# Twelve attention units laid out anew inside GEMM slots, with mask, peak and sink in one VectorE pass

## The reference, cut to what matters

```python
def swa_sink_attention(q, k, v, sinks):
    ...
    s = jnp.einsum('bnqhgd,bnkhd->bnhgqk', qb, kband).astype(jnp.float32) * (dh ** -0.5)
    ...
    s = jnp.where(valid[None, :, None, None, :, :], s, -jnp.inf)
    sink = sinks.astype(jnp.float32).reshape(Hkv, G)[None, None, :, :, None, None]
    m = jnp.maximum(jnp.max(s, axis=-1, keepdims=True), sink)
    p = jnp.exp(s - m)
    p = p / (jnp.sum(p, axis=-1, keepdims=True) + jnp.exp(sink - m))
    o = jnp.einsum('bnhgqk,bnkhd->bnqhgd', p.astype(v.dtype), vband)
```

## Time and profile before

| | |
|---|---|
| Time, median of 3 runs | 2092.64 us (2091.4 to 2093.52) |
| Profiled execution, its own time | 2083.9 us |
| Profiled execution, span | 2082.0 us |
| PE busy | 2015.3 us (97%) |
| DVE busy | 896.3 us (43%) |
| ACT busy | 813.9 us (39%) |
| Clock granted to PE over the span | 0.989 of full speed |

### The profile page before, as it was taken

One profiled execution on the slowest core, in us unless ns is written; L12 is line 12 of the kernel. 1 busy time (PEld: TensorE's weight loads), 2 busy tenths in 40 slices (PEclk: granted clock), 3 DMA queues, 4 the chain that ended last, 5 costly groups with the idle time before them and its releaser, 6 DMA issues.

```text
span 2082.0 us, 28124 instructions
## 1 busy us (share of the span) xinstructions
PE 2015.3 (97%) x12048; PEld 1747.4 (84%) x12048; DVE 896.3 (43%) x1078; ACT 813.9 (39%) x1223; POOL 21.4 (1%) x29
## 2 busy tenths in 40 slices
PE   8999999999999999999999999999997699999998
PEld 6798888787898788889897888899896488888898
DVE  3466265554443233543535333322666453333333
ACT  4442232544333332553545323322565552333321
POOL 0000000000000000000000000000000000000000
PEclk9999999999999999999999999999999799999999
DMA  6422122112242222331122222232222013222222
GB/s 172 139 82 65 57 81 102 61 61 102 81 168 95 94 89 101 109 125 61 62 82 73 99 101 100 90 113 102 94 82 79 1 61 108 90 96 101 101 102 82
DMA packets 29781, 190.67 MB, mean 92 GB/s; under 512 B 3689, under 2 KB 4841, under 8 KB 8562
## 3 DMA queue, kind: packets, MB, share of 16 engines
q1 hardware_dynamic: 26562, 178.58, 24.7%
q0 software_dynamic: 3120, 10.62, 1.9%
HBM read 185.38 MB, written 3.67 MB: 91 GB/s over the span
## 4 chain that ended last, share of the span: by engine, by line
PE 92%; ACT 4%; DVE 3%; issue 1%; POOL 0%; DMA 0%; SPq 0%; POOLq 0%
PE PS L466 27%; PE PS L468 27%; PE PS L467 27%; ACT whi L1286 1%; PE PS L802 1%; PE PS L599 1%; PE PS L616 1%; DVE wlo L1926 1%; PE PS L939 1%; PE PS L780 1%; PE PS L1130 1%; ACT slg L1801 1%; PE PS L1141 1%; PE PS L791 0%; PE PS L736 0%
## 5 line engine op out<-in xcount | busy, mean ns | idle before, releaser
L466 PE MATMUL PS<-hhi,whi 128*128 128x512 f32 x1408 | 563.3, 400 | 9.3 <-POOL small L2586 4.8
L468 PE MATMUL PS<-hhi,wlo 128*128 128x512 f32 x1408 | 554.3, 394 | 0.0
L467 PE MATMUL PS<-hlo,whi 128*128 128x512 f32 x1408 | 550.9, 391 | 0.0
L1926 DVE TENSOR_TENSOR wlo<-raw,whi 128x2048 fp32r<-128x2048 f32 (+1 forms) x119 | 269.5, 2265 | 389.1 <-ACT whi L1286 388.6
L1286 ACT ACTIVATE whi<-raw 128x2048 fp32r<-128x2048 f32 (+2 forms) x166 | 314.9, 1897 | 187.5 <-PE PS L468 187.4
L466 PEld LDWEIGHTS PS<-hhi,whi 128*128 128x128 f32 x1408 | 264.6, 188 | 71.1 <-issue 10.1
L467 PEld LDWEIGHTS PS<-hlo,whi 128*128 128x128 f32 x1408 | 264.5, 188 | 60.6 <-issue 1.9
L468 PEld LDWEIGHTS PS<-hhi,wlo 128*128 128x128 f32 x1408 | 264.5, 188 | 59.6
L466 PE MATMUL PS<-whi,ahi 128*128 128x256 f32 x704 | 194.3, 276 | 0.0
L467 PE MATMUL PS<-wlo,ahi 128*128 128x256 f32 x704 | 194.3, 276 | 0.0
L468 PE MATMUL PS<-whi,alo 128*128 128x256 f32 x704 | 194.3, 276 | 0.0
(11 more groups left out here) (404 smaller groups left out, 3100.1 us busy)
## 6 DMA issues: line engine op xcount, KB each, us to landing
raw<-in_stream SPq DMA_DIRECT2D x165, 1024.0 KB, 4.8
gpost<-in_gposts POOLq DMA_DIRECT2D x5, 512.0 KB, 6.9
X<-in_x SPq DMA_DIRECT2D x4, 512.0 KB, 5.6
X<-in_x POOLq DMA_DIRECT2D x1, 2048.0 KB, 10.5
out<-X SPq DMA_DIRECT2D x4, 512.0 KB, 2.9
bias_line<-linet POOLq DMA_DIRECT2D x1, 1536.0 KB, 35.1
tbias<-bias_line POOLq DMA_DIRECT2D x1, 1024.0 KB, 6.5
memx<-in_mem POOLq DMA_DIRECT2D x1, 1024.0 KB, 5.3
```

Source lines behind the costliest of these rows:

```text
L466: nc.tensor.matmul(out, lh, rh, start=(k == 0), stop=False)
L467: nc.tensor.matmul(out, lh, rl, start=False, stop=False)
L468: return nc.tensor.matmul(out, ll, rh, start=False, stop=(k == n_k - 1))
L1926: V_.tensor_tensor(wlo[:, s % 2, :, cols_], raw[:, s % 2, :, cols_], whi[:, s % 2, :, cols_], ALU.subtract)\
```

## The change

Every hook position is halved in size: `beside` is called eight times in a slot (every 12 matmuls of 256 columns). The work of units 0 to 8 and the logits of units 9 and 10 stand at such sites in the slots Q2 to MV. Logits now stand up to two units ahead of the turn. In the tail only turn and values of units 9 to 11 and the logits of unit 11 are left, and the memory heads, whose second pair is issued head by head. `peaks` is one instruction with an accumulated minimum for each of the four pieces of a unit, where it was two to four instructions over the whole unit and one small one for the sink; it writes the negated masked logits, and `exps` turns the sign back with its scale of -1. Unit 1 gets a buffer of its own, `slg_first`. On DVE and ACT several `split` calls stand at other places: `passed()` before `rotate_sums` of the keys, `split(n + 1)` behind a step of a unit where it was part of the slot's copy.

```diff
-        slg = [slg0, slg1]
+        slg = [slg0, slg_first] + [slg0, slg1] * 5
...
@@ gemm_tokens (gemm_features: "beside" at i % 2 == 0, site 4 * g + i // 2)
+                        if beside and i % 4 == 0:
+                            beside(2 * t + i // 4)
...
@@ PE
+            def beside_second_queries(site):
+
+                if site == 5:
+                    turn_rotated(sqra)
+                elif site == 7:
+                    w.next(S["rot_copied"], 2)
+                    logits(0)
+
+            def beside_values(site):
+
+                if site == 1:
+                    logits(1)
+                elif site == 6:
+                    turn(0)
+
+            def beside_third_queries(site):
+
+                if site == 0:
+                    logits(2)
+                elif site == 1:
+                    values(0)
+                    turn_rotated(skr)
+                elif site == 2:
+                    logits(3)
+                    turn(1)
+                    w.next(S["rot_copied"], 2)
+                    turn_memory_half(0)
+                elif site == 3:
+                    values(1)
+                elif site == 4:
+                    logits(4)
+                    turn(2)
+                elif site == 5:
+                    w.next(S["hlo_ready"], 4)
+                    turn_memory_half(4)
+                    values(2)
+                elif site == 7:
+                    turn(3)
+                    logits(5)
...
+            def beside_memory_keys(site):
+
+                if site == 0:
+                    values(6)
+                    logits(9)
+                elif site == 2:
+                    turn(7)
+                elif site == 6:
+                    values(7)
+                elif site == 7:
+                    logits(10)
...
-            turn(6)
-            logits(7)
+            turn(9)
             stored()
-            memory_logits(0)
-            values(6)
-            turn(7)
-            logits(8)
-            values(7)
-            turn(8)
-            logits(9)
+            first_memory_logits()
+            values(9)
+            logits(11)
+            turn(10)
             memory_turn(0)
-            values(8)
+            values(10)
             memory_turn(1)
-            turn(9)
-            logits(10)
+            w.next(S["mpt_ready"])
+            later_memory_logits(2)
+            w.next(S["mpt_ready"])
             memory_values(0)
-            values(9)
-            memory_logits(1)
-            turn(10)
-            logits(11)
-            values(10)
             turn(11)
+            w.next(S["mo_copied"])
+            later_memory_logits(3)
+            values(11)
             memory_turn(2)
-            values(11)
             memory_turn(3)
+            w.next(S["mpt_ready"], 2)
             memory_values(1)
...
@@ ACT, from MQ's copy to the tail
+            store_features(mqb, 0, MEM_HD ** -0.5)
+            turned(7)
+            exps(9)
+            output(7)
             output_pair(0, 7)
+            store_features(mk2, 0, tokens=M, splits=False)
+            turned(8)
+            split(n + 1)
+            exps(10)
+            output(8)
+            store_tokens(mv2, 0, tiles=2, splits=False)
+            turned(9)
+            split(n + 1)
+            output(9)
             memory_exps(0)
-            turned(7)
-            exps(8)
-            output(7)
+            turned(10)
             memory_exps(1)
-            turned(8)
-            exps(9)
-            output(8)
             memory_turned(0)
+            exps(11)
             memory_turned(1)
...
@@ DVE, peaks
-                half, h = u % 2, SWA_ORDER[2 * (u // 2)]
-                l_, ps_ = slg[half], PS[:, 4:6, :].rearrange("p i (t c) -> p i t c", t=2)
-                peak = nmax[:, half, :].rearrange("p (i t) -> p i t", i=2)
-                if half:
-                    w.link(V_.tensor_tensor(l_[:, :, :, :], ps_, swa.unsqueeze(1).unsqueeze(1).broadcast_to([P, 2, 2, C]), ALU.add))
-                    w.link(V_.tensor_reduce(peak, l_[:, :, :, :], AX.X, ALU.max, negate=True))
...
+                half = u % 2
+                for i in range(2):
+                    h = SWA_ORDER[2 * (u // 2) + i]
+                    for t in range(2):
+                        k0, j = 0 if half or t else P, 2 * i + t
+                        last = V_.tensor_tensor_reduce(slg[u][:, i, t, k0:], PS[:, 4 + i, t * C + k0:(t + 1) * C], swa[:, k0:],
+                                                       -1.0, nsink[:, h:h + 1], ALU.add, ALU.min, nmax[:, half, j:j + 1])
+                last.then_inc(S["lg_ready"], 1)
```

More of the change, by code:

```diff
@@ L484, in gemm_features @@
                             between(g, i // 4)
+                        if beside and i % 2 == 0:
+                            beside(4 * g + i // 2)
                         if arrival and g == 0:
@@ L1155, in values, with memory_logits, first_memory_logits, later_memory_logits @@
                 last.then_inc(S["pv_psum"], 1)
[L1157 to L1166, removed]
+            def memory_logits(h, t):
+                r = slice(MEM_HD * (h % 2), MEM_HD * (h % 2) + MEM_HD)
+                return nc.tensor.matmul(PS[:, 2 * (h % 2) + t // 2, (t % 2) * C:(t % 2) * C + M],
+                                        mqb[r, h // 2, t * P:t * P + P], mk2[r, h // 2, :], start=True, stop=True)
+            def first_memory_logits():
+                for t in range(NT):
+                    memory_logits(0, t)
+                    last = memory_logits(1, t)
+                last.then_inc(S["mlg_psum"], 2)
+            def later_memory_logits(h):
+                for t in range(NT):
+                    last = memory_logits(h, t)
+                last.then_inc(S["mlg_psum"], 1)
             def memory_turn(h):
@@ new lines, in beside_memory_queries @@
+            def beside_memory_queries(site):
+                if site == 0:
+                    values(3)
+                elif site == 1:
+                    turn(4)
+                elif site == 2:
+                    logits(6)
+                    values(4)
+                    turn_rotated(sqra)
+                elif site == 3:
+                    logits(7)
+                    turn(5)
+                elif site == 5:
+                    values(5)
+                    w.next(S["rot_copied"], 2)
+                    logits(8)
+                elif site == 6:
+                    turn(6)
@@ L1188, in _ @@
             w.next(S["rot_copied"], 2)
-            gemm_tokens(bhi, blo, between=lambda t: turn_rotated(sqra) if t == 3 else None)
-            w.next(S["rot_copied"], 2)
+            gemm_tokens(bhi, blo, beside=beside_second_queries)
             value_slot = m
[L1192 to L1225, removed]
-                        turn(4)
-                        logits(5)
-                elif not late:
-                    turn_rotated(sqra)
@@ L2517, in _ @@
+            spread(0)
+            rotate_products(sq[:, 1], key_slot + 2)
+            spread(1)
+            passed()
+            rotate_sums(skr[:, :, :], 2)
+            peaks(2)
             norm_memory(memxb)
             passed()
[L2519 to L2528 removed]
```

179 lines of the change are left out of this document (85 added, 94 removed).

## The result

The changed kernel takes 2062.26 us (median of four, 2052.71 to 2064.8), the kernel before in the same runs 2093.08 us (2091.4 to 2094.21): a ratio of 0.984, 95% interval 0.981 to 0.987, 31 us faster. L numbers of the changed kernel are its own: turns are L1147, logits L1136, values L1159, memory turns L1188, memory logits L1166, memory values L1196, `peaks` L2525.

The account below looks back on a forecast made before the run. The tail was taken to be bound by a chain through PE, DVE and ACT, 10 us a unit. Tail -34.1 and slots +8.5 give -25.6 us, from 2092.6 to 2067 us, range 2057 to 2079.

Parts of the forecast that it names:

- The mechanism: In the old tail, logits(u+1) stand behind turn(u), so a unit takes 10 us; PE's idle time also halves its clock.
- The tail's -34.1: From MV's last matmul to the projection: 28.2 us schedule plus 4 for half clock, 32.2 instead of 66.3.
- The slots' +8.5: Stretch Q1 to MV: 97.1 us grows to 105.6 by moved work, resumptions and new waits, less old idle time and half clock.
- moved steps: In the slots: turns 2.5, values 2.6 and logits 3.8 us move in from the tail, 8.9 us in all.
- eight more resumptions: In the slots: places where the GEMM resumes grow from 16 to 24, at 0.28 us each, 2.2 us.
- new waits: In Q1, Q3, MQ and MV: PE waits for skr 1.1 us and at later steps; sum 4 us, taken as 3.
- The pass: In peaks: 2.3 us for an odd unit, 2.0 for an even one, saving 0.3 to 0.4 us a unit.
- Memory logits: In the tail: PE's memory logits of one head priced at 1.05 us.
- Half rate: Rival, chance 0.17: the pass in peaks runs at half rate, +5 us, 2072 us.
- Waits inside the slots: Rival, chance 0.16: half of 24 places in the slots wait, 16 us instead of 3, +13, 2080 us.
- Slower through `peaks`: Rival, chance 0.04: DVE fills the slots from 4.7 us a unit; gain gone at 1.7 us a pass; 2116 us at 2.2.
- No change: Rival, chance 0.04: the tail keeps its 10 us a unit and the slots give the rest back, 2092 us.

Follow-up runs that it names:

- the four tail kernels: Kernel before, old slots and units kept, only the order behind the last slot changed (one also with new peaks): 2096.91, 2101.33, 2091.99 and 2085.89 us.
- the last kernel: Changed kernel with the keys' rotation sums ahead of the split and the split of the projection's second slot behind the whole tail: 2055.25 us, ratio 0.983.

## Why the prediction was right, and where it was not

The forecast was 2067 us; the measured 2062.26 lies in the range of 2057 to 2079 and the sign is right. The sum said -25.6 us, the timed medians say -30.8, the stretch -30.9: the sum was 5.3 us short, 4.2 of them in the slots and 1.1 in the tail.

**The mechanism** (logits behind the turn make a unit cost 10 us, PE pays again in clock) held: the waits for `spread`, 19.6 us, are 0. But the statement "the unit's chain is broken by the order itself" was too easy. The order of all three engines makes the ring. With the logits ahead on PE and some of DVE's and ACT's steps changed too, three of the four tail kernels only moved the wait. Beside the order, that the units left the tail was needed.

**The tail's -34.1** measured -35.2. The hand schedule, 28.2 us from MV's last matmul to the projection, compares with 28.5 in the last kernel's execution at full clock. On the way turn(10) was due to end at 5.8 and ended at 5.7, turn(11) 17.3 and 16.9. The half clock was sized at 4 us and cost 2.6 (31.1 against 28.5).

**The slots' +8.5** measured +4.3, the larger part of the miss, with every term but the old idle time sized too large. Its terms, from start to start in PE's timelines:

| term | predicted | measured |
|---|---|---|
| moved steps | 8.9 | 8.0 (side work 22.3, without the old half clock, to 30.3) |
| eight more resumptions | 2.2 | 1.2 (GEMM matmuls 69.3 to 70.4) |
| old idle time | -4.0 | -4.0 |
| old half clock | -1.6 | -1.5 |
| new waits | 3.0 | 0.6 |

The 0.28 us of a resumption came from one stretch, behind turn(0) and logits; over the eight new ones it is 0.15 each. Of the seven new waits that I found only the first is there, for `skr`, 0.6 us (up to 1.8 in the other kernels with this order) where I had 1.1. The others, all behind ACT and DVE in Q3, MQ and MV, assumed `peaks` at 2.0 to 2.3 us: with the old peaks two such waits do appear, for `output` (0.6 us) and for `spread` (0.5 in two places).

**The pass** was the step that failed. I took 2.3 us for an odd unit within bounds of 1.9 and 2.7; it took 1.63, below my lower bound. The bound's 0.39 us for the pass itself was near the 0.405 measured, but I added 0.09 for the accumulator's read, which on DVE lies beside the next pass, and then went up from the bound towards passes that don't overlap. "The fusion gives 0.3 to 0.4 us a unit and only where `peaks` ends a wait: one unit in the tail" had the place right for the tail, where peaks(11) gives 1.0 us. It left out the slots, where the old `peaks` makes PE wait 1.1 us for `output` and `spread`: their absence I had put under the order. In the old kernel, where `peaks` stands in the ring, the pass gives 10.9 us.

**Memory logits** were priced at 1.05 us a head. Those of one head, issued alone, take 1.99 us, and those of two heads, issued in turns, 2.00 (rows above; 64 partitions of input each). The first pair therefore came near the planned 2.1, and each later head at twice its price. Little of it reached the sum: the first memory values began 0.5 us behind their copy on ACT (ready at 1622.1, begun at 1622.65), and behind the last head ACT waited 0.85 us for its peaks.

**The rivals.** Half rate: out; 0.405 us a pass and 1.02 ns a column are full rate. The Trainium skill (Vector Engine (DVE) Microarchitecture Reference, § 7, Points that are easy to get wrong) halves the rate for two SBUF sources that aren't bf16; with one source in PSUM the runs here show no such loss. Waits inside the slots: 0.6 us instead of the rival's 16. Slower through `peaks`: the direction is real, the bound was wrong, since I counted DVE's busy time only: PE waited before DVE was full, for the logit banks above all at four times the passes, and paid again in clock. The estimate is 1.2 us a pass, not 1.7. No change: out.

**What the profile should show**: tail 28 to 36 us (31.1), PE busy over 60% of it (75%), waits for `spread` under 5 us (0), a wait of about 1 us before `skr` (0.6), all as said; slots 103 to 109 us (101.3) and the pass at 0.4 to 0.6 (0.405, the low edge) not quite.

## What to carry to other kernels

A chain through several in-order engines is opened only when on no engine a ready step of one unit stands behind a step of the other that still waits: check the ring on each engine's program before you trust a move on one of them. Even then the gain can be small (here 4 us of 31); to put the units between other work that PE has anyway gave the rest. A cheaper instruction in such a ring can give more than it saves there, if the clock follows (7.2 us in a tail with five units at 0.8 to 1.0), and waits that it prevents don't show in the profile of the kernel that has it, so undo it alone to see its worth, and take out what varies by itself. The room for a slower step is set by the waits that its latency brings, which begin before the engine is full.

## What was not expected of the hardware

**The clock fell in a dense stretch, in some executions only.** In the first block's attention, far ahead of the change, the profiled execution of the changed kernel runs at half clock for 10 us, with PE busy before and in it; the kernel before, with the same instructions there, doesn't. Busy time, clock:

```profile
220.00:243.00 23.00, 22.65 (x152) 1.00 0.14 47
243.00:253.00 10.00, 10.00 (x41) 0.50 0.00 0
```
```profile
243.00:253.00 10.00, 10.00 (x61) 1.00 0.00 0
```

It costs 4.8 us. Of the 12 profiled executions of the experiments, whose kernels don't differ there, eight show it too and four don't.

**Two paces at the same granted clock.** The same projection took 43.8 us in five of the 14 profiled executions and 45.5 to 45.7 in eight, with the clock at 1.00 (in the last, 47.5 us, its first 10 us had a clock of 0.78). A window of 7.3 us in it, of the changed kernel and of the one with the sums first:

```profile
1654.50:1661.80 7.30, 7.30 (x67) 7.30 (x66) 2.28 (x1) 0.00 (x0) 0.00 (x0) 1.00 0.40 144
```
```profile
1649.40:1656.70 7.30, 7.30 (x64) 7.30 (x64) 2.29 (x1) 0.33 (x1) 0.00 (x0) 1.00 0.40 146
```

67 matmuls against 64, 4% apart, with the same code. Both paces also stand in one execution: in slot Q1, before and after the change, matmuls start 0.118 us apart up to the transposes of `skr` and 0.113 behind them. In the feed-forward loop that starts at 1117 us of its span the changed kernel's execution is the slower one, 22.4 us for each of ten rounds where that of before took 22.0 (matmuls of 512 columns 0.233 us apart, or 0.2286). The clock and this pace are why the span of the changed kernel's profile is only 22.9 us shorter: 9.6 us were lost ahead of Q1. What sets the pace isn't known.
